# Norms, pooling and routing between a dense FFN and its experts: tile-by-tile order with combined affine rows

## What is computed

```python
# layer 0: gated DeltaNet mixer, 8 heads; k is normalised per head and token
k = k * rsqrt(sum(k * k, -1) + EPS)
...
x = layer_norm(ALPHA * x + g1 * y, ln_g[0, 0], ln_b[0, 0])
y = swiglu(x * (1 + sc2) + sh2, ffn_w_gu, ffn_w_down)        # dense FFN
x = layer_norm(ALPHA * x + g2 * y, ln_g[0, 1], ln_b[0, 1])
# layer 1: pooling mixer, then 8 experts, top 2
h = x * (1 + sc1) + sh1
y = (einsum(pool(h), w_grp) + b_grp) * scale                 # pool: 4 channel groups, windows 2/4/8/16
x = layer_norm(ALPHA * x + g1 * y, ln_g[1, 0], ln_b[1, 0])
h = x * (1 + sc2) + sh2
probs = softmax(h @ router_w)
top_p, top_i = top_k(probs, 2); top_p = top_p / sum(top_p)
y = sum over e of gates[e] * swiglu(h, w_gu[e], w_down[e])
x = layer_norm(ALPHA * x + g2 * y, ln_g[1, 1], ln_b[1, 1])
```

## Time and profile before

| what | us |
|---|---|
| median of 3 runs (2387.28 to 2397.77) | 2390.71 |
| the profiled execution, its own time | 2393.28 |
| span of its instructions | 2391.4 |
| PE busy in the span | 2037.4 (85%) |
| DVE busy | 1050.0 (44%) |
| ACT busy | 744.4 (31%) |
| POOL busy | 778.7 (33%) |

### The profile page before, as it was taken

The page is one execution under the profiler, slowest core; times in us unless marked ns, Lnnn a source line. Parts: engine busy times, 40 slices in busy tenths (PEclk is TensorE's granted clock), DMA queues, the critical chain, the costliest instruction groups (busy, mean ns, idle before and its releaser), DMA issues.

```text
span 2391.4 us, 40168 instructions
## 1 busy us (share of the span) xinstructions
PE 2037.4 (85%) x14398; PEld 1546.4 (65%) x14399; DVE 1050.0 (44%) x1655; ACT 744.4 (31%) x1201; POOL 778.7 (33%) x482
## 2 busy tenths in 40 slices
PE   4999999999997889998999924368998898899990
PEld 2546777677766458886888723346777677687770
DVE  2204555566655453323122279455333733633226
ACT  0112333233322012221222000055455645554331
POOL 0006323443233031111111143265444734643224
PEclk7899999999998999999999966579999999999995
DMA  7113233322323433233223212178566857856343
GB/s 240 53 45 117 74 98 101 116 79 82 92 88 96 166 113 105 80 125 112 92 84 115 82 45 79 69 248 271 172 192 210 272 177 223 271 174 199 106 155 145
DMA packets 252696, 320.71 MB, mean 134 GB/s; under 512 B 21223, under 2 KB 192495, under 8 KB 252487
## 3 DMA queue, kind: packets, MB, share of 16 engines
q1 hardware_dynamic: 236823, 282.78, 37.2%
q10 hardware_dynamic: 11632, 20.11, 2.3%
q0 software_dynamic: 4032, 14.68, 1.6%
HBM read 284.91 MB, written 32.59 MB: 133 GB/s over the span
## 4 chain that ended last, share of the span: by engine, by line
PE 59%; issue 16%; POOL 12%; DVE 8%; DMA 2%; ACT 2%; ACTq 0%; SPq 0%; POOLq 0%; DVEq 0%
POOL wlo L1233 11%; PE pp L1082 9%; PE pp L1084 9%; PE pp L1083 9%; PE pp L699 8%; PE pp L683 3%; PE pp L615 3%; PE pp L804 2%; PE pp L837 2%; PE pp L703 2%; PE pp L717 2%; PE pp L1027 1%; PE pp L830 1%; DVE x L2138 1%; DVE x L2135 1%
## 5 line engine op out<-in xcount | busy, mean ns | idle before, releaser
L1233 POOL TENSOR_TENSOR wlo<-wring,whi 128x1024 fp32r<-128x1024 f32 x182 | 440.0, 2423 | 805.4 <-ACT whi L1661 749.7
L1082 PE MATMUL pp<-whi,xTh 128*128 128x512 f32 (+1 forms) x1152 | 449.3, 390 | 35.0 <-POOL wlo L1233 25.3
L1661 ACT ACTIVATE whi<-wring 128x1024 fp32r<-128x1024 f32 (+1 forms) x328 | 320.0, 983 | 468.0 <-PE pp L1084 359.3
L2203 DVE TENSOR_TENSOR wlo<-wring,whi 128x1024 fp32r<-128x1024 f32 x182 | 286.4, 1575 | 344.0 <-ACT whi L1661 279.9
L1084 PE MATMUL pp<-wlo,xTh 128*128 128x512 f32 (+1 forms) x1152 | 434.9, 378 | 0.3 <-issue 0.3
L1083 PE MATMUL pp<-whi,xTl 128*128 128x512 f32 (+1 forms) x1152 | 435.0, 378 | 0.0
L1082 PEld LDWEIGHTS pp<-whi,xTh 128*128 128x128 f32 x1152 | 221.0, 192 | 85.9 <-issue 24.6
L1084 PEld LDWEIGHTS pp<-wlo,xTh 128*128 128x128 f32 x1152 | 220.8, 192 | 41.0 <-issue 0.7
L1083 PEld LDWEIGHTS pp<-whi,xTl 128*128 128x128 f32 x1152 | 221.6, 192 | 35.4
L1082 PE MATMUL pp<-whi,hTh 128*128 128x512 f32 x528 | 213.5, 404 | 18.7 <-POOL wlo L1233 9.9
L699 PE MATMUL pp<-xT,wring 128*128 128x512 f32 x384 | 206.9, 621 | 2.6 <-ACT scratch L1469 2.0
(11 more groups left out here) (279 smaller groups left out, 2760.3 us busy)
## 6 DMA issues: line engine op xcount, KB each, us to landing
wring<-in_moe_w_gu SPq DMA_DIRECT2D x320, 256.0 KB, 3.7
wring<-in_ada_w SPq DMA_DIRECT2D x80, 512.0 KB, 4.6
wring<-in_moe_w_down SPq DMA_DIRECT2D x160, 256.0 KB, 3.4
wring<-in_ffn_w_gu SPq DMA_DIRECT2D x80, 256.0 KB, 3.1
wring<-in_dn_w_in SPq DMA_DIRECT2D x96, 128.0 KB, 3.7
wring<-in_ffn_w_down SPq DMA_DIRECT2D x40, 256.0 KB, 2.9
expert_in<-zeros SPq DMA_DIRECT2D x36, 256.0 KB, 3.2
wring<-in_ada_w SPq DMA_DIRECT2D x32, 256.0 KB, 5.6
```

Source lines behind the costliest of these rows:

```text
L1082: pe.matmul(out, hi[:, c0 + c, tt], wh, start=(first and c == 0), stop=False)
L1233: pool.tensor_tensor(wlo[:, hs, :, 0:w], wring[:, ring_p.slot(k), 0:2, 0:w], whi[:, hs, :, 0:w].bitcast(F32), ALU.subtract).then_inc(slot_ ...
L1661: act.activation(whi[:, hs, 0:nk, 0:w], wring[:, ring_v.slot(k), 2 * s:2 * s + nk, 0:w], ACT.Copy)\
L2203: dve.tensor_tensor(wlo[:, hs, 0:nk, 0:w], wring[:, ring_v.slot(k), 2:2 + nk, 0:w], whi[:, hs, 0:nk, 0:w].bitcast(F32), ALU.subtract).then ...
```

## The change

It has four parts.

1. **DeltaNet.** The k squares are made from the transposed tile: PE transposes first, ACT squares the result out of PSUM (`k_squares`), DVE sums along the tile with a reduction (`k_sums`). The five ones-matmuls of k are gone; those of q stay.
2. **Combined rows.** During the FFN, SP loads the modulation rows and norm rows of the middle in pieces of 8 elements (32 bytes) per partition (`raw`), DVE combines them in 11 small instructions (`mid_rows`), and SP writes 15 rows to DRAM (`combo_dram`) from where they are broadcast. An affine of the norm and an affine of the modulation become one: `hrow` comes straight from the statistics by two instructions (`affine`). Pool scale and gate are multiplied into two copies of the pool weights on POOL, and the pool bias enters as a matmul of one row (L1225).
3. **Order of the middle.** Statistics are taken in `add_y` itself; DVE walks tiles in a staggered order (`pool_input`, `pool_residual`, `expert_input`), POOL only makes the roots, and the router runs tile by tile. `x` is brought to its final form (`affine` into `x`) after routing and is parked tile by tile from SP. The first expert weights are loaded and split earlier.
4. **Routing.** Softmax division is dropped (gates follow from the top two exponentials), prefix sums go in three steps over padded rows in place of seven or nine, and waits stand only where data need them. Ranks and totals come from ten matmuls.

```diff
-                    square_sums(h + 1, 0, PP[3][:, 0:T], free=True)
                     k_tokens(h + 1)
...
+            def k_squares(h):
+                act.wait_ge(S["tok_ps"], 2 * h + 1)
+                if h:
+                    act.wait_ge(S["ss_ps"], h)
+                act.activation(sq[:, 0:NT], PP[2][:, 0:NT], ACT.Square).then_inc(S["sq_done"], 1)
...
             def k_sums(h):
-                dve.wait_ge(S["ss_ps"], 2 * h + 1)
-                dve.tensor_scalar(ss[:, 0, :], PP[3][:, 0:T], EPS, None, ALU.add).then_inc(S["ss_done"], 1)
+                dve.wait_ge(S["sq_done"], 2 * h + 1)
+                dve.tensor_reduce(ss[:, 1, :], per_tile(sq[:, 0:NT]), AX.X, ALU.add).then_inc(S["ksum"], 1)
+                dve.wait_ge(S["ksum"], h + 1)
+                dve.tensor_scalar(ss[:, 0, :], ss[:, 1, :], EPS, None, ALU.add).then_inc(S["ss_done"], 1)
...
+                if e:
+                    dve.wait_ge(S["ffn_res"], i + 1)
+                    dve.bn_stats(lnst[:, t, a, :], x[:, t, cols]).then_inc(S["ln_step"], 1)
...
+            def affine(dst, t, first, second, signal, done):
+                dve.scalar_tensor_tensor(dst, x[:, t, :], lnmv[:, t, 0:1], first, ALU.subtract, ALU.mult).then_inc(S[signal], 1)
+                dve.wait_ge(S[signal], done - 1)
+                dve.scalar_tensor_tensor(dst, dst, rstd[:, 1, t:t + 1], second, ALU.mult, ALU.add).then_inc(S[signal], 1)
...
+            def pool_residual(t):
+                xt = x[:, t, :]
+                dve.scalar_tensor_tensor(xt, xt, lnmv[:, t, 0:1], ag_row, ALU.subtract, ALU.mult).then_inc(S["x2_step"], 1)
...
+                dve.wait_ge(S["pool_ps"], t + 1)
+                dve.scalar_tensor_tensor(xt, xt, rstd[:, 1, t:t + 1], PP[2 + t % 2][:, :], ALU.mult, ALU.add).then_inc(S["x2_step"], 1)
...
+            for t in range(3):
+                last_y(t)
+            pool_input(0)
+            last_y(3)
+            pool_input(1)
+            last_y(4)
+            pool_input(2)
+            pool_residual(0)
+            pool_input(3)
...
+            pool_product(0)
+            pool_product(1)
+            for t in range(T):
+                pool_linear(t)
+                if t + 2 < T:
+                    pool_product(t + 2)
...
+                for a in range(2):
+                    pe.matmul(out[:, 512 * a:512 * a + 512], cm[0:1, ONES, :], pool_bias[1 if t else 0][:, 512 * a:512 * a + 512],
+                              start=True, stop=False)
...
+            for t in range(T):
+                expert_columns(t)
+                if t:
+                    router(t - 1)
+            router(T - 1)
...
+                for k in range(2):
+                    ins = pool.tensor_tensor(w[:, :, k, :], w[:, :, k, :], gs, ALU.mult)
+                ins.then_inc(S["pw_scaled"], 1)
...
+                    sp.wait_ge(S["combo_step"], 11)
+                    sp.dma_start(combo_dram.rearrange("r (p i) -> p r i", p=P), combo).then_inc(S["raw_in"], 16)
...
+            dve.wait_ge(S["a2_in"], 32)
+            for t in range(T):
+                affine(x[:, t, :], t, x2_rows[:, 0, :], x2_rows[:, 1, :], "x2_step", 2 * T + 2 * t + 2)
...
-                    act.dma_start(xpark.rearrange("(t p) d -> p t d", p=P), x[:, :, :]).then_inc(S["x_parked"], 16)
...
+            for t in range(T):
+                sp.wait_ge(S["x2_step"], 2 * T + 2 * t + 2)
+                sp.dma_start(xpark[t * P:(t + 1) * P, :], x[:, t, :]).then_inc(S["x_parked"], 16)
```

More of the change, by code:

```diff
@@ L555, in parts, with moe_fill @@
                 return [quarters(dst[:, 4 * a:4 * a + 4, :], wp[:, 4 * a:4 * a + 4, :]) for a in range(2)]
+            for k in range(2):
+                for half, pieces in enumerate(parts(ring.slot(k))):
+                    for split in slot_split[0]:
+                        sp.wait_ge(split, 37 + k)
+                    for dst, src in pieces:
+                        sp.dma_start(dst, src).then_inc(slot_loaded[ring.slot(k)][half], 16)
+            ring.base += 2
+            def moe_fill(e, k):
+                expert_fill(1, e, k, gu1[e] if isinstance(e, int) else gu1[bass.ds(e, 1)].rearrange("a k n -> (a k) n"),
+                            A["moe_w_down"][0][e] if isinstance(e, int) else
+                            A["moe_w_down"][0][bass.ds(e, 1)].rearrange("a f d -> (a f) d"), (0, FE))
@@ L556, in _ @@
             for split in slot_split[0]:
                 sp.wait_ge(split, 36 + RING)
-            for half, pieces in enumerate(parts(ring.slot(0))):
-                for dst, src in pieces:
-                    sp.dma_start(dst, src).then_inc(slot_loaded[ring.slot(0)][half], 16)
-            ring.base += 1
-            sp.wait_ge(S["ln_step"], T * LN_STEPS)
-            for r in range(2):
-                row_load(rows[:, r, :], mod_dram[1, r, 2 * D:3 * D], "rows_in")
-            row_load(rows[:, 2, :], A["ln_g"][1, 0], "rows_in")
@@ L566, in _ @@
[L566 to L574 removed]
+            moe_fill(0, 0)
@@ L575, in _ @@
+            for k in range(3, 18):
+                moe_fill(0, k)
+            with sp.Fori(1, 8) as e:
+                for k in range(18):
+                    moe_fill(e, k)
             ring.base += 144
@@ L1222, in _ @@
             pool.memset(zeros[:, :], 0.0).then_inc(S["pool_const"], 1)
+            pool.memset(before[:, :, :, :], 0.0)
+            pool.memset(cnt[:, :, 0:8], 0.0)
+            pool.memset(cnt[:, 0, 16:24], 1.0)
+            for i in range(T):
+                ins = pool.memset(marks[:, :, i], P * i + 0.5 if i else -0.5)
+            ins.then_inc(S["pool_const"], 1)
             pool.wait_ge(S["pool_const"], 1)
@@ L2296, in expert @@
                                 dve.wait_ge(S["ln0_x"], 2 * T)
-                            add_y(e, m // 6)
+                            for t in range(T):
+                                add_y(e, m // 6, t)
                         if m >= 2 and l:
@@ L2341, in _ @@
+            pool_input(3)
+            pool_residual(1)
+            pool_input(4)
+            pool_residual(2)
+            expert_input(0)
+            pool_residual(3)
+            expert_input(1)
+            pool_residual(4)
+            for t in range(2, T):
+                expert_input(t)
             step = [0]
@@ new lines, in _ @@
+            rsync()
+            assert step[0] <= ROUTE_SEL, step[0]
+            dve.sem_inc(S["route_step"], ROUTE_SEL - step[0])
+            step[0] = ROUTE_SEL
+            dve.wait_ge(S["once_ps"], 6 + T)
+            rank, total = bank(5)[:, 0:40].rearrange("p (t e) -> p t e", t=T), bank(5)[:, 40:48]
+            over = flat[:, 320:360].rearrange("p (e i) -> p e i", e=8)
+            rts(dve.tensor_tensor(over, total.rearrange("p (e o) -> p e o", o=1).to_broadcast([P, 8, T]), marks[:, :, :], ALU.is_gt))
```

522 lines of the change are left out of this document (276 added, 246 removed).

## The result

The changed kernel takes **2335.6 us** (2333.2 to 2337.9), the kernel before 2391.5; the ratio is 0.9765, with a 95% interval of 0.9745 to 0.9785. It is faster, as forecast, but by 56 us and not by 91: 2300 was forecast, with a range of 2284 to 2322, and the time lies 14 us above it. The profiled execution of the changed kernel has a span of 2331.4 us.

A forecast was written before the change was run, and what follows sets the result against it. The middle, from FFN to experts, was taken as a 206.8 us stretch of engines waiting for one another. Terms -87.8, -3.9, +2.3, +2.7 and -4.0 sum to -90.7 us: 2300 us forecast, range 2284 to 2322.

The forecast's parts named there:

- the experts' stage keeps its length: From the experts' first product to the end: no change; a changed length was named as showing the forecast wrong.
- DVE idle in the middle for more than 10 us: Sign in the middle, between FFN and experts: such idling of DVE would show the forecast wrong.
- The middle up to the router's end: From the first last-column `add_y` to the router's end: 73 us in place of 160.8, -87.8 us.
- The 1520 window: Old trace's router: PE counts as busy at clock 0.50, taken as speaking against a warm router for 8-column products.
- Routing: From the router's end to the first scatter: 12.8 us in place of 16.7, -3.9 us (bounds -6.6 and -3).
- Scatter to experts: From the first scatter to the experts' first product, 29.3 us before: +2.3 us (bounds -2.3 and +5).
- the parks' collision: During the scatter: SP's parking of x, 2.6 MB, competes for the DMA engines, taken at +4.6 us, up to 7.
- FFN: Statistics in `add_y(1, 0)` slow DVE, so PE waits longer in the last columns: four steps of 0.67, +2.7 us.
- DeltaNet: Heads without k's ones-matmuls: about 0.7 us saved per head, seven times, less head 0: -4.0 us (bounds -8 and +2).
- The 1 us that head 0 was to cost: In DeltaNet's first head, which has no slack for the longer norm chain: 1 us lost.
- Rival (a): PE stays at 1.2 GHz and binds the middle; router ends near 107 in place of 73: 2334 us, chance 0.10.
- Rival (b): Experts' start gives back 14 us through full park collision, late first product and waits for splits: 2314 us, chance 0.10.

The follow-up runs named there:

- N = 1: The changed kernel with one single one-column copy added on ACT ahead of its expert loop: 2300.4 us.
- N = 8: The changed kernel with eight one-column copies added on ACT ahead of its expert loop: 2296.6 us, ratio 0.9619.
- a shift of 1: ACT's expert loop begins one instruction later than in the changed kernel, through one added copy: 2300.4 us.
- the run with both edits: Changed kernel plus eight ACT copies, x parked before its last affine step, unread wide PE products in router, before rank product and first expert: 2287.1 us.

## Why the prediction was wrong, step by step

- **The step that failed** is one that the sum gave no term: that the experts' stage keeps its length. The prediction named this as a sign of its failure, but held no case for it and gave no reason for putting it at nothing. (Its other sign, DVE idle in the middle for more than 10 us, came as well: 13.7 us behind the router.) It costs 34.1 us, almost the whole of the miss (35.6 us), because ACT's loop over the experts had moved by one instruction and was fetched anew each time round. With N = 1 and N = 8 the same kernel takes 2300.4 and 2296.6 us, beside the forecast 2300. That nearness is partly luck: the other terms miss by +5.4, -2.3, +0.7, -0.4 and -2.7 us and cancel, and 4.1 us come from the pieces that aren't listed.
- **The middle up to the router's end:** right in kind, 5.4 us short. DVE's own work and its first wait came as worked out: it ends at 64.7 (63 forecast), and `pool_residual(0)` waits 3.97 us (4). Its four waits come to 8.2 us in place of 6, which leaves 56.5 us for its own work, as forecast; the second wait is 2.52 us where 1 was taken, behind a group product of 5.41 us in place of 3.72 during 3 us of low clock. The router was mis-sized: I took 73, between 68 (full clock) and 77 (low clock), and it is 78.4, since the clock is 0.50 from tile 2 on. The 1520 window had spoken against a warm router, and taken at its word it gives the 77. The rule of the Trainium skill that was weighed against it ("TensorE: Matmul & The Clock Gate", Part 1: The HAM clock gate: activity releases the throttle) doesn't hold for the changed kernel's router, busy throughout its last 16 us and at 0.50; with wide products among the narrow ones the clock stayed, and the router took the 71.4 us.
- **Routing:** 10.5 us, where 12.8 was forecast; -6.2 lies inside the bounds of -3 and -6.6. DVE waits 4.6 us for the rank product, which was taken at 5.3, and the rest is that pairs of small instructions that don't wait for each other start 0.11 us apart, where 0.23 was taken for each.
- **Scatter to experts:** 32.3 us, 31.6 forecast. Two terms were off and cancel in part: the parks' collision is 6.0 in place of 4.6 us, and from the token load to the product it takes 8.7 us, where 9.4 was forecast.
- **FFN:** +2.3, +2.7 forecast. The size fits, the place is shown only in part: of PE's waits in the last columns, which were to grow by 2.7 us, the profile names one, at tile 2, and it grows from 3.34 to 4.38.
- **DeltaNet:** a head in 75.23, as forecast (75.3); seven steps give 5.6 to 6.7 us. The 1 us that head 0 was to cost would lie ahead of the first of these instants, where runs of one kernel differ by 3 us, so it can't be told. The path is the forecast's, a longer chain on DVE that uses up PE's slack: PE now starts 0.06 us behind the end of the scaling, where it had 2.7. DVE and PE in the changed kernel:

```profile
400.73 0.82 DVE L2000 TENSOR_TENSOR big<-pp,ss 128x640 f32<-128x640 f32 x1 [1.28 <-POOL ss L1326]
401.61 0.77 PE L773 MATMUL pp<-cm,big 128*128 128x128 f32 x5
```

  The working was loose, though: its own instants, 406.9 against 407.36, give 0.5 us a head and not the 0.7 that it used, and 0.8 was measured.
- **Rival (a)**, PE at the low clock, gave 2334 us, which is the measured time, by the wrong way: the pooling ran as forecast and only the router was cold. A number that fits shows no mechanism. **Rival (b)** placed a give-back at the experts' start, 14 us at the most. Its first part nearly came (a collision of 6.0 us, 7 at the most), the rest did not: the large waits for splits come at every expert's end, behind ACT.
- **The range:** the bounds that the terms print add up to 2314 at the upper end, or 2317 with SP's issues uncovered, and not to 2316. None of these reaches 2335.6. (The first piece of the old middle ends at 1425.2 us; the 1423.93 given for it is the start of its last instruction. No term uses it.)

## What to carry to other kernels

Where a loop runs on an engine beside others, any edit ahead of it on that engine, be it one instruction, can move it across a fetched piece and change a stage that the edit doesn't touch. So compare the count of instruction packets in the two pages first, then look for an engine that stands still at the loop's branch with nothing to wait for; if both are there, shift the loop by a few instructions before you judge the change. A forecast for such a kernel needs a case for it. And work that is not needed early is best put where its engine waits anyway: taken out of the time in which the DMA engines were full, it gave 6 us and cost none.

## What the runs showed of the hardware

- Code comes in packets of 8 KB, and the effect of a loop's place repeats every 128 instructions. A loop on ACT of 339 listed instructions repeats without a fetch if it begins at the right place (0 to between 15 and 43 instructions behind the edge that a shift of 1 crosses), and otherwise is fetched anew each time round, five to six packets, with a stop of 7 to 12.5 us at the branch in place of 3. One instruction more or less made 37 us of the experts' stage (847.5 and 810.1).
- The granted clock stayed at 1.00 through products of 8 columns when wide products ran between them, and at 0.50 without those, with PE busy throughout. After 21 us of wide products and a gap of 3 us it was still 1.00, but fell 2 us into the next work, in which PE waited again (in the run with both edits, at 1467 us).
- The DMA engines took 389 GB/s for 16 us with scatter and parks together; with parks out of the way the token load was issued 6.0 us sooner behind the first scatter.
